# Attention to the 16 meta keys: one joint transpose and one block-diagonal product per block of 128 queries, instead of one small transpose and one small product per head

## The chip, the cores and the metric

The kernel runs on one core of a Trainium2 chip. The metric is the device time of one execution, in microseconds (us); lower is better. A core has TensorE (matmul, in the profile PE, its weight loads PEld), VectorE (DVE), ScalarE (ACT), GpSimd (POOL), and SyncE (SP), which starts most DMAs. Each engine works through its own list in order and waits on semaphores that the others raise.

## The reference

One hybrid decoder layer on 512 tokens of width 1024, with 16 learned meta tokens ahead of them: sliding-window attention (8 query heads, 2 key heads, head size 64, window 128), gated linear attention beside it, a gated merge, and a mixture of 32 experts. The change touches only this part of the attention:

```python
s_band = einsum('bnqhgd,bnkhd->bnhgqk', qb, k_band) * scale     # 128 queries x 256 keys of the band
s_meta = einsum('bnqhgd,bmhd->bnhgqm', qb, k_meta) * scale      # 128 queries x 16 meta keys
p = softmax(concatenate([s_meta, s_band, sink], axis=-1))
o = einsum('bnhgqk,bnkhd->bnqhgd', p_band, v_band) + einsum('bnhgqm,bmhd->bnqhgd', p_meta, v_meta)
```

## The kernel before

The 512 tokens are four blocks (b = 0 to 3) of 128 queries. A pair (b, i) with i = 0 to 3 stands for two query heads j = 0, 1 of block b, one for each key head; there are 16 pairs, numbered n = 4b + i. One list of steps, `SCHEDULE` (L189 to L254), is walked by all the engines, each doing its own part of every step in that order. In the stretch that holds the attention, it lays the steps of the pairs between 24-matmul units of a large projection (chunks 10 to 17 of the weights, two units each, `unit`; their weights are split in two halves by `prep`, ACT L1233 and DVE L1547; their results go through an exponential on ACT, L1320, and `sig` on DVE, L1699 and L1700). For pair n the order is: unit, then `PV` of pair n-2, `S` of pair n, `PT` of pair n-1, sometimes `ogT` and `oT` (transposes of outputs), then `sig`.

- `S` (L838): TensorE multiplies queries by keys, 272 columns for a head (128 keys of the block before, 16 meta keys, 128 own keys, and the meta keys' scores again behind; block 0 has 144). DVE adds the mask and takes the maximum (L1721, L1726). ACT takes the exponential (L1364, L1366) and leaves the head's probabilities in one of four buffers `prob`.
- `PT` (L851): TensorE transposes the probabilities of the two heads, for each head the 128 columns of the block before (L860, not in block 0), the 128 own columns (L861) and the 16 meta columns (L862). ACT copies head 0 out of PSUM (L1378 the band, L1379 the meta part), DVE copies head 1 (L1738, L1739). The meta part goes into `ptm`, a 128x128 tile whose rows 16 to 127 are zero.
- `PV` (L863): per head one product with the values of the block before (L873), one with the own values (L874), one of `ptm` with the meta values (L877), all added up in the head's 64 columns of one PSUM bank. After i = 3, `onorm` scales the block (DVE L1744 to L1749).

PSUM banks are dealt out by `Banks.take` (L129): every family of steps has a ring of banks, and TensorE waits until the earlier use of a bank has been read. The family "T" (L426), which the transposes of `PT` use, has two banks, 5 and 6: head 0 takes one, head 1 the other. ACT takes the exponentials of `S` of pair n before the copies of `PT` of pair n-1, since this is the order of the list.

Of the kernel before, what the change touches and what calls it, by code (L numbers as in the profile page):

```python
# [21 lines left out]
ALU = mybir.AluOpType  # L22
ACT = mybir.ActivationFunctionType
# [4 lines left out]
T = 512  # L28
P = 128
NB = T // P  # L30
KT = D // P
NM = 16
XC = NM + T
HQ, HKV, DH = 8, 2, 64
# [10 lines left out]
SLOT = 64  # L45
# [23 lines left out]
LOGITS = 2 * NG + NE  # L69
# [6 lines left out]
CST = {}  # L76
_o = 0
for _n, _w in (("ident", 128), ("mask", 288), ("cc", NB * DH), ("ss", NB * DH), ("ccm", DH), ("ssm", DH),
               ("slots", SLOT), ("pad", LOGITS), ("att_mask", 128), ("tok", NB + 1)):
    CST[_n] = (_o, _o + _w)  # L80
    _o += _w
NCST = _o
# [2 lines left out]
def shape_tables():  # L85

    c = np.zeros((P, NCST), np.float32)

    def put(name, value):
        a, b = CST[name]  # L90
        c[:value.shape[0], a:b] = value.reshape(value.shape[0], -1)

    i, j = np.arange(P)[:, None], np.arange(P)[None, :]
    put("ident", np.eye(P, dtype=np.float32))
    prev = np.where(j > i, 0.0, NEG)
    own = np.where(j <= i, 0.0, NEG)
    put("mask", np.concatenate([prev, np.zeros((P, NM)), own, np.zeros((P, NM))], 1).astype(np.float32))
    half = DH // 2
    inv = np.float32(10000.0) ** (-(np.arange(half, dtype=np.float32) * np.float32(2.0)) / np.float32(DH))

    def angles(pos):
        a = pos.astype(np.float32)[..., None] * inv
        return (np.concatenate([np.cos(a), np.cos(a)], -1), np.concatenate([-np.sin(a), np.sin(a)], -1))

    cc, ss = angles(NM + np.arange(T).reshape(NB, P).T)
    put("cc", cc)
    put("ss", ss)
    cc, ss = angles(np.arange(NM))
    put("ccm", cc)
    put("ssm", ss)  # L110
    put("slots", np.tile(np.arange(1, SLOT + 1, dtype=np.float32), (P, 1)))
    put("att_mask", ((i <= j) & (i // GC == j // GC)).astype(np.float32))
    pad = np.zeros((P, LOGITS), np.float32)
    pad[:, NG:2 * NG] = -3.0e38
    put("pad", pad)
    put("tok", np.concatenate([np.tile(np.arange(NB, dtype=np.float32) * P - 2 * T, (P, 1)), i.astype(np.float32)], 1))
    return c


# [69 lines left out]
def schedule():  # L189
# [28 lines left out]
    def product(n):  # L218
        b, i = pairs[n]
        return [("PV", b, i)] + ([("onorm", b)] if i == 3 else [])  # L220

    for c in range(10, 18):
        s += [("prep", c + 1)]
        for u in range(2):
            n = 2 * (c - 10) + u
            b, i = pairs[n]
            s += [("unit", c, u)] + (product(n - 2) if n >= 2 else [])
            s += [("S", b, i)] + ([("PT",) + pairs[n - 1]] if n >= 1 else [])
            if i == 2:
                s += [("ogT", b)] + ([("oT", b - 1)] if b >= 1 else [])  # L230
            s += [("sig", c, u)]
    s += [("prep", 19), ("unit", 18, 0)] + product(14) + [("PT",) + pairs[15], ("unit", 18, 1)] + product(15)
    s += [("unit", 18, 2), ("oT", NB - 1), ("unit", 18, 3)]
    s += [("prep", 20)] + [("unit", 19, u) for u in range(4)]
    s += [("prep", 21), ("unit", 20, 0), ("prep", 22), ("unit", 20, 1), ("unit", 20, 2), ("prep", 23), ("unit", 20, 3), ("hi", 24)]
# [22 lines left out]
def layer_kernel(nc, x, meta_tokens, norm1_w, w_in, q_norm_w, k_norm_w, attn_sinks, gla_gate_up, gla_gate_bias,  # L258
                 gla_norm_w, w_attn_branch, w_gla_branch, w_out, norm2_w, router_rows, norm2_rows,
                 expert_w_gate, expert_w_up, expert_w_down, table, triangle, rows_hbm, out):  # L260
    with ExitStack() as ctx:
# [3 lines left out]
        def sem(name):  # L265
            return ctx.enter_context(nc.semaphore(name))
# [19 lines left out]
        def C(name, rows=P):  # L286
            a, b = CST[name]
            return cst[0:rows, a:b]
# [7 lines left out]
        def at(name, offset, shape, dt=F32):  # L296
            size = int(np.prod(shape[1:])) * 4
            assert offset + size <= arena_size, (name, offset, size, arena_size)
            return nc.alloc_sbuf_tensor_at(name, shape, dt, offset=arena_start + offset)
# [43 lines left out]
        vgm = at("vgm", Y + 14 * K1, [NM, 512])  # L343
        oghi = at("oghi", Y, [P, 4, T], F32R)
        oglo = at("oglo", Y + 8 * K1, [P, 4, T], F32R)
        ptm = [at(f"ptm{i}", 81 * K1 + 512 * i, [P, P]) for i in range(2)]
        place = [Y + 16 * K1]

        def more(name, shape, dt=F32):
# [91 lines left out]
        s_set2 = sem("gate_rows_set")  # L441
        s_reset = sem("chunk_starts_set")
        s_vm0 = sem("meta_values_cleared")
        s_pad = sem("meta_probs_cleared")
        s_sumsq = sem("x_squares_summed")
        s_mean = sem("x_means")
        s_rstd = sem("x_rstd")
# [113 lines left out]
        def head_before(n, k):  # L561

            m = n - k
            return (m // 8, m % 8 // 2, m % 2)
# [39 lines left out]
        def _(pe):  # L604
# [71 lines left out]
            for step in SCHEDULE:  # L676
# [174 lines left out]
                elif kind == "PT":  # L851
                    _, b, i = step
                    n0 = 2 * (4 * b + i)
                    for j in range(2):
                        pe.wait_ge(s_prob, n0 + j + 1)
                        ps = banks.take(pe, "T", ("PT", b, i, j))
                        p = prob[(n0 + j) % 4]
                        own = KW if b else 0
                        if b > 0:
                            nc.tensor.transpose(ps[:, 0:128], p[:, 0:128], ident)  # L860
                        nc.tensor.transpose(ps[:, 128:256], p[:, own:own + P], ident)  # L861
                        nc.tensor.transpose(ps[0:NM, 256:384], p[:, P:KW], ident).then_inc(banks.done(("PT", b, i, j)), 1)  # L862
                elif kind == "PV":  # L863
                    _, b, i = step
                    if i == 0:
# [1 line left out]
                    for j in range(2):  # L867
                        pe.wait_ge(*banks.emptied(("PT", b, i, j)))
                        hd = j * 4 + i
                        o = pv[:, hd * DH:(hd + 1) * DH]  # L870
                        vc = slice(j * DH, (j + 1) * DH)
                        if b > 0:
                            nc.tensor.matmul(o, pt[j][:, 0:128], v_tok[:, b - 1, vc], start=True, stop=False)  # L873
                        nc.tensor.matmul(o, pt[j][:, 128:256], v_tok[:, b, vc], start=(b == 0), stop=False)  # L874
                        if i == 0 and b == 0:
                            pe.wait_ge(s_pad, 2)
                        last = nc.tensor.matmul(o, ptm[j][:, :], vm[:, vc],  # L877
                                                start=False, stop=True)
                    last.then_inc(s_pv, 1)
                elif kind in ("oT", "ogT"):  # L880
                    b = step[1]
# [308 lines left out]
        def _(act):  # L1190
# [29 lines left out]
            for step in SCHEDULE:  # L1220
# [147 lines left out]
                elif kind == "PT":  # L1368
# [2 lines left out]
                    act.wait_ge(*banks.filled(name))  # L1371
                    if 4 * b + i:
                        act.wait_ge(s_pv, 4 * b + i)
                    else:
                        act.wait_ge(s_pad, 1)
                    ps = banks.get(name)
                    c0 = 128 if b == 0 else 0
                    nc.scalar.activation(pt[0][:, c0:256], ps[:, c0:256], ACT.Copy)  # L1378
                    nc.scalar.activation(ptm[0][0:NM, :], ps[0:NM, 256:384], ACT.Copy).then_inc(banks.read(name), 1)  # L1379
                elif kind in ("oT", "ogT"):  # L1380
                    b = step[1]
                    act.wait_ge(*banks.filled(step))
# [93 lines left out]
        def _(dve):  # L1476
# [59 lines left out]
            for step in SCHEDULE:  # L1536
# [171 lines left out]
                elif kind == "S":  # L1708
# [3 lines left out]
                    for j in range(2):  # L1712
                        n = 2 * (4 * b + i) + j
                        hd = j * 4 + i
                        name = ("S", b, i, j)
                        st_ = att_stat[:, b % 2, :, hd:hd + 1]
                        width, m0 = keys(b)[1], 0 if b else KW
                        dve.wait_ge(*banks.filled(name))
                        if n >= 4:
                            dve.wait_ge(*banks.filled(("PT",) + head_before(n, 4)))  # L1720
                        nc.vector.tensor_tensor_reduce(out=prob[n % 4][:, 0:width], in0=banks.get(name)[:, 0:width],  # L1721
                                                       in1=C("mask")[:, m0:m0 + width], scale=1.0, scalar=-3.0e38,
                                                       op0=ALU.add, op1=ALU.max, accum_out=st_[:, 0, :])\
                            .then_inc(banks.read(name), 1)
                        dve.wait_ge(*banks.emptied(name))
                        nc.vector.tensor_scalar(st_[:, 1, :], st_[:, 0, :], -SCALE, nsinks[:, hd:hd + 1],  # L1726
                                                ALU.mult, ALU.min).then_inc(s_max, 1)
                elif kind == "PT":
# [2 lines left out]
                    dve.wait_ge(*banks.filled(name))  # L1731
                    if 4 * b + i:
                        dve.wait_ge(s_pv, 4 * b + i)
                    else:
                        dve.wait_ge(s_pad, 2)
                    ps = banks.get(name)
                    c0 = 128 if b == 0 else 0
                    nc.vector.tensor_copy(pt[1][:, c0:256], ps[:, c0:256])  # L1738
                    nc.vector.tensor_copy(ptm[1][0:NM, :], ps[0:NM, 256:384]).then_inc(banks.read(name), 1)  # L1739
                elif kind == "onorm":  # L1740
                    b = step[1]
                    st_ = att_stat[:, b % 2, :, :]
# [179 lines left out]
        def _(pool):  # L1922
# [31 lines left out]
            for step in SCHEDULE:  # L1954
# [18 lines left out]
                elif kind == "krope":  # L1973
# [9 lines left out]
                    for g in range(HKV):  # L1983
# [7 lines left out]
                    rope(m, tabm[:, 0:1, :].to_broadcast([NM, HKV, DH]), tabm[:, 1:2, :].to_broadcast([NM, HKV, DH]),  # L1991
                         view(n_x, NM, HKV), view(n_t, NM, HKV), krm[:, :].rearrange("p (g d) -> p g d", d=DH),
                         NM, HKV, s_krope, 2)
                elif kind == "kT":
                    pool.wait_ge(*banks.emptied("kdm"))
                    for t in ptm:
                        nc.gpsimd.memset(t[:, :], 0.0).then_inc(s_pad, 1)
                elif kind == "qrope":
                    b = step[1]
                    pool.wait_ge(*banks.emptied(("unit", 6, b)))  # L2000
# [89 lines left out]
```

## Time and profile before

| | |
|---|---|
| Median of 3 runs | 671.71 us (671.52 to 671.83) |
| Span of the profiled execution | 669.8 us |
| Median less span (start and end outside the span) | 1.9 us |
| TensorE busy | 650.2 us, 97% |
| TensorE weight loads busy | 466.9 us, 70% |
| VectorE busy | 390.7 us, 58% |
| ScalarE busy | 215.9 us, 32% |
| GpSimd busy | 101.4 us, 15% |

The page gives the span of the profiled execution, not a separate time of its own; the 1.9 us between it and the median of the runs is what lies around the span. In timelines, a row with xN holds N instructions one behind another. A float32 matmul appears as two matmul instructions (x2). Matmuls overlap, so what one costs in a stream is the distance from its start to the start of the next, not its duration.

### The profile page before, as it was taken

How to read it: one execution, taken by the hardware profiler on the slowest of the kernel's cores; microseconds unless marked ns; L12 is line 12 of the kernel's file. 1: busy time of each engine (PE TensorE's matmuls, PEld its weight loads, DVE VectorE, ACT ScalarE, POOL GpSimd, SP SyncE). 2: the span in 40 equal slices, each digit the busy share in tenths (PEclk: the TensorE clock that was granted, in tenths of full speed). 3: DMA queues.
4: the chain of work that ended last, by engine and by line, in shares of the span. 5: the costliest groups of instructions: out<-in, count | busy, mean ns of one | idle time of the engine just before them, and what ended most of it. 6: DMA issues, size and time to landing. Idle time of an engine off the chain costs nothing.

```text
span 669.8 us, 10196 instructions
## 1 busy us (share of the span) xinstructions
PE 650.2 (97%) x3969; PEld 466.9 (70%) x3969; DVE 390.7 (58%) x736; ACT 215.9 (32%) x448; POOL 101.4 (15%) x138
## 2 busy tenths in 40 slices
PE   5799999999999999999989999999999999999998
PEld 3579999988888888888779995354544445453535
DVE  4648335678897878785674667453443535251615
ACT  6346232234534444422435565302020201110112
POOL 3300015899300000000000010110110101010010
PEclk9899999999999999999999999999999999999999
DMA  7432223202232121112345057999999999999943
GB/s 242 147 125 65 64 65 97 92 1 64 79 100 74 60 68 52 68 44 90 126 166 243 33 219 284 381 408 412 401 422 397 423 394 420 407 418 404 417 185 126
DMA packets 49794, 138.72 MB, mean 207 GB/s; under 512 B 6202, under 2 KB 28235, under 8 KB 41556
## 3 DMA queue, kind: packets, MB, share of 16 engines
q1 hardware_dynamic: 47298, 134.37, 52.8%
q0 software_dynamic: 2304, 3.64, 1.5%
q8 instruction: 32, 0.52, 0.3%
q14 instruction: 14, 0.11, 0.1%
q10 hardware_dynamic: 146, 0.07, 0.0%
HBM read 138.62 MB, written 4.19 MB: 213 GB/s over the span
## 4 chain that ended last, share of the span: by engine, by line
PE 87%; DVE 6%; ACT 3%; issue 2%; DMA 1%; POOL 0%; ACTq 0%; DVEq 0%
PE bank L990 16%; PE bank L608 12%; PE bank L609 12%; PE bank L610 12%; PE bank L1004 8%; PE bank L1114 8%; PE bank L850 1%; DVE y_lo L1903 1%; PE bank L1015 1%; PE bank L877 1%; PE bank L874 1%; ACT whi L1233 1%; DVE sig_a L1617 1%; DVE sig_a L1613 1%; DMA wraw<-in_w_out 1%
## 5 line engine op out<-in xcount | busy, mean ns | idle before, releaser
L990 PE MATMUL bank<-w_pair,xgT 128*64 128x512 f32 x512 | 113.8, 596 | 0.0
L990 PEld LDWEIGHTS bank<-w_pair,xgT 128*64 128x64 f32 x512 | 35.2, 137 | 66.4 <-issue 65.4
L1547 DVE TENSOR_TENSOR wlo<-wraw,whi 128x2048 fp32r<-128x2048 f32 (+1 forms) x25 | 56.4, 2258 | 20.3 <-ACT whi L1233 20.3
L608 PE MATMUL bank<-whi,xhi 128*128 128x256 f32 x224 | 64.4, 288 | 0.0
L609 PE MATMUL bank<-wlo,xhi 128*128 128x256 f32 x224 | 63.0, 281 | 0.0
L610 PE MATMUL bank<-whi,xlo 128*128 128x256 f32 x224 | 62.9, 281 | 0.0
L608 PE MATMUL bank<-xhi,whi 128*128 128x512 f32 x152 | 61.4, 404 | 0.0
L609 PE MATMUL bank<-xlo,whi 128*128 128x512 f32 x152 | 60.1, 396 | 0.0
L610 PE MATMUL bank<-xhi,wlo 128*128 128x512 f32 x152 | 59.7, 393 | 0.0
L1004 PE MATMUL bank<-w_pair,hT 128*64 128x512 f32 x256 | 58.1, 595 | 0.0
L1880 DVE SCALAR_TENSOR_TENSOR hg<-bank,pair_w,hs 128x256 f32<-128x256 f32 x16 | 7.7, 483 | 80.6 <-ACT hs L1452 80.6
L1233 ACT ACTIVATE whi<-wraw 128x2048 fp32r<-128x2048 f32 (+1 forms) x25 | 46.6, 1870 | 24.9 <-PE bank L617 11.1
L1452 ACT ACTIVATE hs<-bank 128x256 f32<-128x256 f32 x16 | 6.1, 384 | 135.5 <-PE bank L990 135.5
L1916 DVE TENSOR_TENSOR h<-h,bank 128x512 f32<-128x512 f32 x64 | 41.4, 681 | 7.5 <-PE bank L1114 6.0
L1114 PE MATMUL bank<-y_hi,onehotT 128*128 128x512 f32 x112 | 44.2, 394 | 1.5 <-DVE y_lo L1903 1.5
L1114 PE MATMUL bank<-y_lo,onehotT 128*128 128x512 f32 x112 | 43.7, 390 | 0.0
L1903 DVE TENSOR_TENSOR y_lo<-bank,y_hi 128x512 fp32r<-128x512 f32 x32 | 20.6, 685 | 39.2 <-ACT y_hi L1465 39.2
L608 PEld LDWEIGHTS bank<-whi,xhi 128*128 128x128 f32 x224 | 42.1, 188 | 1.8 <-issue 1.4
L610 PEld LDWEIGHTS bank<-whi,xlo 128*128 128x128 f32 x224 | 42.2, 188 | 0.0
L609 PEld LDWEIGHTS bank<-wlo,xhi 128*128 128x128 f32 x224 | 42.1, 188 | 0.0
L1004 PEld LDWEIGHTS bank<-w_pair,hT 128*64 128x64 f32 x256 | 17.7, 137 | 33.3 <-issue 33.3
L1927 POOL TENSOR_TENSOR pause<-pause 128x1 f32<-128x1 f32 x34 | 6.0, 196 | 223.0 <-PE bank L984 184.1
(331 smaller groups left out, 1330.9 us busy)
## 6 DMA issues: line engine op xcount, KB each, us to landing
w_pair<-in_expert_w_gate SPq DMA_DIRECT2D x32, 1024.0 KB
w_pair<-in_expert_w_up SPq DMA_DIRECT2D x32, 1024.0 KB
w_pair<-in_expert_w_down SPq DMA_DIRECT2D x32, 1024.0 KB, 17.4
wraw<-in_w_in SPq DMA_DIRECT2D x17, 1024.0 KB, 5.6
wraw<-in_w_out SPq DMA_DIRECT2D x4, 1024.0 KB, 5.3
h<-in_x SPq DMA_DIRECT2D x4, 512.0 KB, 5.3
wraw<-in_w_gla_branch SPq DMA_DIRECT2D x2, 1024.0 KB, 5.0
wraw<-in_w_attn_branch SPq DMA_DIRECT2D x2, 1024.0 KB, 5.2
```

The source lines that it names most:

```text
L608: nc.tensor.matmul(ps, lhi(k), rhi(k), start=(k == 0), stop=False)
L609: nc.tensor.matmul(ps, lhi(k), rlo(k), start=False, stop=False)
L610: last = nc.tensor.matmul(ps, llo(k), rhi(k), start=False, stop=(k == kt - 1))
L850: nc.tensor.matmul(ps[:, 0:width], q, k, start=True, stop=True).then_inc(banks.done(("S", b, i, j)), 1)
L990: last = nc.tensor.matmul(tiles[GU_BANK[s]][j * SLOT:(j + 1) * SLOT, :].rearrange("p (f n) -> p f n", f=2), xgT[:, k, s * P + j * SLOT:s * ...
L1004: last = nc.tensor.matmul(tiles[DOWN_BANKS[s][half]][j * SLOT:(j + 1) * SLOT, :], hT[s][:, f, j * SLOT:(j + 1) * SLOT], we[s][j][2][:, f, ...
L1114: last = nc.tensor.matmul(tiles[SCATTER_BANKS[u % 4]][:, :], onehotT[i % 3][s][:, b, :], part[s][:, cols_], start=(s == 0 and part is y_hi ...
L1233: nc.scalar.activation(wh, raw, ACT.Copy).then_inc(s_hi, 1)
L1547: nc.vector.tensor_tensor(wl, raw, wh.bitcast(F32), ALU.subtract).then_inc(s_lo, 1)
L1880: nc.vector.scalar_tensor_tensor(hg[s][:, :], tiles[GU_BANK[s]][:, FF:2 * FF], pair_w[:, 2 * i + s:2 * i + s + 1], hs[s][:, :], ALU.mult, ...
L1903: last = nc.vector.tensor_tensor(y_lo[s][:, cols_], tiles[DOWN_BANKS[s][half]][:, :], y_hi[s][:, cols_].bitcast(F32), ALU.subtract)
L1916: nc.vector.tensor_tensor(h[:, b, cols_], h[:, b, cols_], tiles[bank][:, :], ALU.add).then_inc(s_add[u % 4], 1)
```

## The change

The 16 meta columns of the probabilities are no longer transposed head by head. GpSimd copies them, as each head's probabilities are ready, side by side into `pm` (128 queries x 8 heads x 16). After `PT` of a block's last pair a new step `metaT` transposes `pm` at once (128x128) through a bank of family "T", and ACT copies it to `pmT`. A block-diagonal matrix `vmb` (128 rows for 8 heads x 16 keys, 512 columns for 8 heads x 64) is built once, by a new step `vmeta`: TensorE repeats the meta values in eight groups of 16 rows, DVE multiplies by a 0/1 table. In `PV` of the last pair, one product of `pmT` with `vmb` adds all eight heads' meta part to the whole bank. The bank's accumulation is started by its first matmul alone. The constants table is 136 columns longer. The buffers `ptm` and their clearing go.

```diff
+    def flip(n):
+        b, i = pairs[n]
+        return [("PT", b, i)] + ([("metaT", b)] if i == 3 else [])
...
-            s += [("S", b, i)] + ([("PT",) + pairs[n - 1]] if n >= 1 else [])
+            s += [("S", b, i)] + (flip(n - 1) if n >= 1 else [("vmeta",)])
...
-    s += [("prep", 19), ("unit", 18, 0)] + product(14) + [("PT",) + pairs[15], ("unit", 18, 1)] + product(15)
+    s += [("prep", 19), ("unit", 18, 0)] + product(14) + flip(15) + [("unit", 18, 1)] + product(15)
...  TensorE
-                        nc.tensor.transpose(ps[:, 128:256], p[:, own:own + P], ident)
-                        nc.tensor.transpose(ps[0:NM, 256:384], p[:, P:KW], ident).then_inc(banks.done(("PT", b, i, j)), 1)
+                        nc.tensor.transpose(ps[:, 128:256], p[:, own:own + P], ident).then_inc(banks.done(("PT", b, i, j)), 1)
+                elif kind == "metaT":
+                    b = step[1]
+                    pe.wait_ge(s_pm, 8 * (b + 1))
+                    ps = banks.take(pe, "T", step)
+                    nc.tensor.transpose(ps[:, 0:P], pm[b % 2][:, :, :], ident).then_inc(banks.done(step), 1)
+                elif kind == "vmeta":
+                    pe.wait_ge(*banks.emptied(("unit", 5, "m")))
+                    ps = banks.take(pe, "T", step)
+                    nc.tensor.matmul(ps[:, 0:P], C("copies", NM), vm[0:NM, :], start=True, stop=True).then_inc(banks.done(step), 1)
...
+                        first = i == 0 and j == 0
                         if b > 0:
-                            nc.tensor.matmul(o, pt[j][:, 0:128], v_tok[:, b - 1, vc], start=True, stop=False)
-                        nc.tensor.matmul(o, pt[j][:, 128:256], v_tok[:, b, vc], start=(b == 0), stop=False)
-                        last = nc.tensor.matmul(o, ptm[j][:, :], vm[:, vc],
-                                                start=False, stop=True)
+                            nc.tensor.matmul(o, pt[j][:, 0:128], v_tok[:, b - 1, vc], start=first, stop=False)
+                        last = nc.tensor.matmul(o, pt[j][:, 128:256], v_tok[:, b, vc], start=first and b == 0, stop=False)
+                    if i == 3:
+                        pe.wait_ge(*banks.emptied(("vmeta",)))
+                        pe.wait_ge(*banks.emptied(("metaT", b)))
+                        last = nc.tensor.matmul(pv[:, :], pmT[:, :], vmb[:, :, :].rearrange("p h d -> p (h d)"), start=False, stop=True)
...  ScalarE
-                    nc.scalar.activation(pt[0][:, c0:256], ps[:, c0:256], ACT.Copy)
-                    nc.scalar.activation(ptm[0][0:NM, :], ps[0:NM, 256:384], ACT.Copy).then_inc(banks.read(name), 1)
+                    nc.scalar.activation(pt[0][:, c0:256], banks.get(name)[:, c0:256], ACT.Copy).then_inc(banks.read(name), 1)
+                elif kind == "metaT":
+                    b = step[1]
+                    act.wait_ge(*banks.filled(step))
+                    if b:
+                        act.wait_ge(s_pv, 4 * b)
+                    nc.scalar.activation(pmT[:, :], banks.get(step)[:, 0:P], ACT.Copy).then_inc(banks.read(step), 1)
...  VectorE
+                            dve.wait_ge(s_pm, n - 3)
...
-                    nc.vector.tensor_copy(pt[1][:, c0:256], ps[:, c0:256])
-                    nc.vector.tensor_copy(ptm[1][0:NM, :], ps[0:NM, 256:384]).then_inc(banks.read(name), 1)
+                    nc.vector.tensor_copy(pt[1][:, c0:256], banks.get(name)[:, c0:256]).then_inc(banks.read(name), 1)
+                elif kind == "vmeta":
+                    dve.wait_ge(*banks.filled(step))
+                    dve.wait_ge(*banks.filled(("glao", NB - 1)))
+                    full = [P, HKV, 4, DH]
+                    nc.vector.tensor_tensor(vmb[:, :, :].rearrange("p (g i) d -> p g i d", g=HKV), ...
+                                            ALU.mult).then_inc(banks.read(step), 1)
...  GpSimd
-                elif kind == "kT":
-                    pool.wait_ge(*banks.emptied("kdm"))
-                    for t in ptm:
-                        nc.gpsimd.memset(t[:, :], 0.0).then_inc(s_pad, 1)
+                elif kind == "S":
+                    _, b, i = step
+                    if i == 0 and b >= 2:
+                        pool.wait_ge(*banks.filled(("metaT", b - 2)))
+                    for j in range(2):
+                        n = 2 * (4 * b + i) + j
+                        pool.wait_ge(s_prob, n + 1)
+                        nc.gpsimd.tensor_copy(pm[b % 2][:, 2 * i + j, :], prob[n % 4][:, P:KW]).then_inc(s_pm, 1)
```

## Rows read from the trace of the kernel before

**Rows 1.** Chain of waits, 160 to 350 us, by line; then a piece of it.
```profile
by line: PE bank L608 17.9%; PE bank L609 17.8%; PE bank L610 17.7%; PE bank L850 5.1%; issue 4.3%; PE bank L877 3.8%; PE bank L874 3.6%; ACT whi L1233 3.0%; DVE sig_a L1617 3.0%; DVE sig_a L1613 2.9%; DMA wraw<-in_w_out 2.8%; DVE wlo L1547
...
306.27 1.93 ACT whi L1233
```

**Rows 2.** Stretches: busy us (instructions) of the engines, PEclk, DMA share, GB/s.
```profile
20.00:30.00 10.00, 9.56 (x35) 6.21 (x36) 6.58 (x6) 0.69 (x3) 5.41 (x9) 0.83 0.69 224
...
250.00:300.00 50.00, 50.00 (x288) 41.49 (x286) 42.55 (x68) 20.12 (x54) 0.00 (x0) 1.00 0.15 51
...
330.00:350.00 20.00, 17.27 (x103) 14.71 (x102) 14.88 (x17) 8.95 (x10) 0.00 (x0) 1.00 0.43 145
```

**Rows 3.** Instructions of L877: minimum, median, maximum ns, first and last start.
```profile
L877 PE MATMUL bank<-kvm,ptm x64: 275/275/275, 180.2 to 299.9; 128*128 128x64 f32 x64
```

**Rows 4.** TensorE's timeline, PV, S and PT at pair 8: start, us, instruction.
```profile
228.69 0.39 PE L877 MATMUL bank<-kvm,ptm 128*128 128x64 f32 x2
228.91 0.39 PE L873 MATMUL bank<-v_tok,pt 128*128 128x64 f32 x2
...
229.67 0.73 PE L850 MATMUL bank<-kT,qT 64*128 64x272 f32 x4
...
230.83 0.27 PE L861 MATMUL bank<-cst,prob 128*128 128x128 f32 x1
230.94 0.27 PE L862 MATMUL bank<-cst,prob 128*16 128x128 f32 x1
```

**Rows 5.** TensorE's timeline, a float32 product of 512 columns and what follows.
```profile
45.55 1.12 PE L750 MATMUL bank<-gdT,gate_up 17*128 17x512 f32 x2
46.51 0.51 PE L757 MATMUL bank<-gdT,gate_up 17*128 17x16 f32 x4
```

**Rows 6.** Timeline of DVE and ACT, the same pair 8.
```profile
230.43 0.44 DVE L1721 CUSTOM_DVE_ANT_0 prob<-bank,cst 128x272 f32<-128x272 f32 x1 [0.62 <-PE bank L850]
...
231.17 0.52 ACT L1364 ACTIVATE prob<-prob,att_stat 128x272 f32<-128x272 f32 x1 [2.07 <-DVE att_stat L1726]
...
231.99 0.27 DVE L1739 COPY ptm<-bank 16x128 f32<-16x128 f32 x1
...
232.57 0.36 ACT L1378 ACTIVATE pt<-bank 128x256 f32<-128x256 f32 x1
```

**Rows 7.** Timeline around pair 4: TensorE, DVE at pairs 3, 4 and 5, ACT.
```profile
197.15 0.27 PE L861 MATMUL bank<-cst,prob 128*128 128x128 f32 x1
...
189.34 0.31 DVE L1721 CUSTOM_DVE_ANT_0 prob<-bank,cst 128x144 f32<-128x144 f32 x1 [0.75 <-PE bank L850]
...
196.98 0.44 DVE L1721 CUSTOM_DVE_ANT_0 prob<-bank,cst 128x272 f32<-128x272 f32 x1 [0.36 <-PE bank L850]
...
204.04 0.69 DVE L1749 TENSOR_TENSOR o_tok<-bank,att_stat 128x512 f32<-128x512 f32 x1 [1.39 <-PE bank L877]
...
199.11 0.26 ACT L1378 ACTIVATE pt<-bank 128x128 f32<-128x128 f32 x1
```

**Rows 8.** Timeline at the last pair: TensorE and ACT.
```profile
295.50 0.27 PE L861 MATMUL bank<-cst,prob 128*128 128x128 f32 x1
...
295.60 0.38 ACT L1378 ACTIVATE pt<-bank 128x256 f32<-128x256 f32 x1 [0.74 <-PE bank L862]
```

**Rows 9.** Timeline at 399 us: a weight load that waits for an ACT copy.
```profile
399.40 0.38 ACT L1396 ACTIVATE xnT<-bank 128x256 f32<-128x256 f32 x1 [0.20 <-PE bank L898]
...
399.84 0.52 PEld L909 LDWEIGHTS bank<-router,xnT 128*128 128x128 f32 x4 [0.22 <-ACT xnT L1396]
```

**Rows 10.** TensorE's timeline, two of its idle times.
```profile
20.44 3.56 PE L636 MATMUL bank<-xhi,gdp 128*48 128x512 f32 x8 [3.91 <-DVE xlo L1565]
...
335.13 0.50 PE L608 MATMUL bank<-ohi,whi 128*128 128x512 f32 x1 [1.10 <-DVE sig_g L1613]
```

**Rows 11.** POOL's timeline, two like operations, the second its last for long.
```profile
166.90 3.23 POOL L1927 TENSOR_TENSOR rgs<-og,rgs 128x512 f32<-128x512 f32 x1
...
172.47 1.28 POOL L1927 TENSOR_TENSOR rgs<-og,rgs 128x512 f32<-128x512 f32 x1
```

More of the change, by code:

```diff
@@ L78 @@
 for _n, _w in (("ident", 128), ("mask", 288), ("cc", NB * DH), ("ss", NB * DH), ("ccm", DH), ("ssm", DH),
-               ("slots", SLOT), ("pad", LOGITS), ("att_mask", 128), ("tok", NB + 1)):
+               ("slots", SLOT), ("pad", LOGITS), ("att_mask", 128), ("tok", NB + 1), ("copies", 128), ("own_head", HQ)):
     CST[_n] = (_o, _o + _w)
@@ L116, in shape_tables @@
     put("tok", np.concatenate([np.tile(np.arange(NB, dtype=np.float32) * P - 2 * T, (P, 1)), i.astype(np.float32)], 1))
+    put("copies", (np.arange(NM)[:, None] == j % NM).astype(np.float32))
+    heads = np.arange(HQ)[None, :]
+    put("own_head", (i // NM == 2 * (heads % 4) + heads // 4).astype(np.float32))
     return c
@@ L345, in layer_kernel @@
         oglo = at("oglo", Y + 8 * K1, [P, 4, T], F32R)
-        ptm = [at(f"ptm{i}", 81 * K1 + 512 * i, [P, P]) for i in range(2)]
+        pm = [at(f"pm{i}", 81 * K1 + 512 * i, [P, HQ, NM]) for i in range(2)]
+        vmb = at("vmb", G + 48 * K1, [P, HQ, DH])
+        pmT = at("pmT", G + 50 * K1, [P, P])
         place = [Y + 16 * K1]
@@ L443, in layer_kernel @@
         s_vm0 = sem("meta_values_cleared")
-        s_pad = sem("meta_probs_cleared")
+        s_pm = sem("meta_probs_kept")
         s_sumsq = sem("x_squares_summed")
@@ L871, in _ @@
                         vc = slice(j * DH, (j + 1) * DH)
+                        first = i == 0 and j == 0
                         if b > 0:
-                            nc.tensor.matmul(o, pt[j][:, 0:128], v_tok[:, b - 1, vc], start=True, stop=False)
-                        nc.tensor.matmul(o, pt[j][:, 128:256], v_tok[:, b, vc], start=(b == 0), stop=False)
-                        if i == 0 and b == 0:
-                            pe.wait_ge(s_pad, 2)
-                        last = nc.tensor.matmul(o, ptm[j][:, :], vm[:, vc],
-                                                start=False, stop=True)
+                            nc.tensor.matmul(o, pt[j][:, 0:128], v_tok[:, b - 1, vc], start=first, stop=False)
[4 more added lines that the diff above has]
+                        last = nc.tensor.matmul(pv[:, :], pmT[:, :], vmb[:, :, :].rearrange("p h d -> p (h d)"), start=False, stop=True)
                     last.then_inc(s_pv, 1)
@@ L1373, in _ @@
                         act.wait_ge(s_pv, 4 * b + i)
-                    else:
-                        act.wait_ge(s_pad, 1)
-                    ps = banks.get(name)
                     c0 = 128 if b == 0 else 0
-                    nc.scalar.activation(pt[0][:, c0:256], ps[:, c0:256], ACT.Copy)
-                    nc.scalar.activation(ptm[0][0:NM, :], ps[0:NM, 256:384], ACT.Copy).then_inc(banks.read(name), 1)
+                    nc.scalar.activation(pt[0][:, c0:256], banks.get(name)[:, c0:256], ACT.Copy).then_inc(banks.read(name), 1)
[5 more added lines that the diff above has]
+                    nc.scalar.activation(pmT[:, :], banks.get(step)[:, 0:P], ACT.Copy).then_inc(banks.read(step), 1)
                 elif kind in ("oT", "ogT"):
@@ L1733, in _ @@
                         dve.wait_ge(s_pv, 4 * b + i)
-                    else:
-                        dve.wait_ge(s_pad, 2)
-                    ps = banks.get(name)
                     c0 = 128 if b == 0 else 0
-                    nc.vector.tensor_copy(pt[1][:, c0:256], ps[:, c0:256])
-                    nc.vector.tensor_copy(ptm[1][0:NM, :], ps[0:NM, 256:384]).then_inc(banks.read(name), 1)
+                    nc.vector.tensor_copy(pt[1][:, c0:256], banks.get(name)[:, c0:256]).then_inc(banks.read(name), 1)
[3 more added lines that the diff above has]
+                    full = [P, HKV, 4, DH]
+                    nc.vector.tensor_tensor(vmb[:, :, :].rearrange("p (g i) d -> p g i d", g=HKV),
+                                            banks.get(step)[:, 0:P].rearrange("p (g d) -> p g d", g=HKV).unsqueeze(2).to_broadcast(full),
+                                            C("own_head").rearrange("p (g i) -> p g i", g=HKV).unsqueeze(3).to_broadcast(full),
+                                            ALU.mult).then_inc(banks.read(step), 1)
                 elif kind == "onorm":
```

## The prediction

> **What bounds the kernel now.** I read the page first (busy shares, slices), then the chain of waits, then TensorE's own waits, then the timeline of one pair of heads. TensorE is busy 97% of the span. In the chain from 160 to 350 us the large units' lines L608 to L610 and the attention's L850, L877 and L874 lead, and up to 306 us every piece is TensorE's own [rows 1]: the reader is to see that nothing else releases it there. The stretches say the same: between 250 and 300 us TensorE is busy 50.00 of 50 us, DVE 42.55, ACT 20.12 [rows 2]. So an instruction more or less on TensorE counts in full, and so does any wait that it gets. Behind 306 us the chain hops between ACT, DVE and DMA, but its first hop, ACT L1233, starts when TensorE ends a unit at 306 [rows 1]; all that follows moves with it. I count the sum on this execution's span, 669.8 us; the median of the runs is 1.9 us above it, and I add the change of the span to the median.
>
> **What TensorE loses.** Of L877 there are 64 instructions, so 32 float32 products, one for each head and block [rows 3]; of L862 there is one transpose for each head and block too, 32. In the stream an L877 product takes from 228.69 to 228.91, that is 0.22 us; a transpose of PT takes from 230.83 (L861) to 230.94 (L862), that is 0.11 us [rows 4], and I take the same for the 16-column ones, which repeat at this distance. Removed: 32 x 0.22 = 7.0 and 32 x 0.11 = 3.5, together 10.5 us.
>
> The Trainium skill (TensorE: Matmul & The Clock Gate, Back-to-back issue gap) prices one matmul of N columns at N/2.4 + 2.5 ns, and with four passes for true float32 (FP8 and Floating Point Precision, TensorE Precision Notes) a 64-column product would be 0.12 us; by that estimate only 3.7 us would go in place of 7.0, and the result would be 3.3 us worse. The trace has 0.22 us, since full weights are loaded for each; it decides.
>
> **What TensorE gains in work.** Four wide products, 128x128 by 512 columns in float32. The nearest row is L750, float32 with 512 columns too: 0.96 us to the next start, with the start of another kind of product behind it included [rows 5]. I take 0.9, since the wide product follows its like: 3.6 us. Bounds: 4 x 0.22 (no dearer than an L877) and 4 x 1.12 (L750's full duration), 0.9 to 4.5. Four `metaT` transposes at 0.11 are 0.4 us. `vmeta`, one product with 128 columns, lies between one and two L877 products, 0.2 to 0.5; I take 0.3. Added: 4.3 us. By work alone the change is worth 10.5 - 4.3 = 6.2 us.
>
> **What TensorE gains in waits.** Family "T" has two banks. PT of pair n-1 takes both, head 0 the one that ACT empties, head 1 the one that DVE empties. Until now the next taker was PT of the next pair, a whole unit later, and found them free. `metaT` is a third taker immediately behind: the ring gives it head 0's bank again (13 uses lie ahead of the attention, `vmeta` makes them 14, each pair adds two, so the parity holds; each `metaT` turns the roles of the banks, but still meets head 0's). TensorE must stand until ACT has copied head 0, and ACT comes to that copy only behind both exponentials of S of pair n, which TensorE issued less than a microsecond before.
> At pair 8 [rows 4, 6]: S starts at 229.67, DVE's maximum at 230.43, the exponentials at 231.17 and 231.88, L1378 from 232.57 to 232.93. PT's last L862 would be over at 230.94 + 0.11; with two transposes less, `metaT` wants to start 0.22 earlier, at 230.83. Wait: 232.93 - 230.83 = 2.1 us. From the end of an ACT copy to the weight load that waited for it, 399.78 to 399.84, are 0.06 us [rows 9]; with this and refilling the pipe 2.2 us. None of the pieces between S and L1378 is removed, so the distance stays.
> Pair 12 repeats pair 8's pattern (two such in all): 2.2.
> At pair 4, whose PT is block 0's (two transposes left, so `metaT` wants 197.15), L1378 ends at 199.37 [rows 7]: 2.2, with the restart 2.3. Here DVE has little slack: it waited 0.75 us for S at pair 3 and 0.36 at pair 4 [rows 7]. TensorE comes faster, by 0.66 us for a pair (two L877, two L862), against 0.27 us less work on DVE, L1739 [rows 6]; at pair 3 it is 1.0 us ahead of before (2 x 0.66, less 0.3 for `vmeta`), at pair 4 the gain and DVE's saving and wait cancel, so DVE comes 0.2 to 0.3 us late. So 2.5.
> At the last pair no S lies ahead. `metaT` wants to start where L861 does now, 295.50. L1378 ran from 295.60 for 0.38 us [rows 8] and would start one transpose (0.11) earlier, ending at 295.87. Wait and restart: 0.5.
> Sum of waits: 2.5 + 2.2 + 2.2 + 0.5 = 7.4 us. Bounds: zero, if the bank were free after all, and 4 x 3.3 (from S to the end of L1378 at pair 8), 13.
>
> Behind the standing `metaT` in TensorE's list are the next unit, PV and S, so all wait; nobody makes the time up, since DVE and ACT only feed on what TensorE delivers there. The wide product itself waits for `pmT`, which has a unit of time: no cost.
>
> **The edits that I cost at nothing.** GpSimd's 32 copies: it is idle from 173.8 us on (its last work there, 172.47 and 1.28 us [rows 11]; 0.00 between 250 and 300 us [rows 2]), and the meta columns of a block's last head are ready a whole pair before `metaT` asks. Cover gone, each copy would stand in the path; a POOL operation took 3.23 us once where its like took 1.28 [rows 11], so 2 us more at a `metaT` is the bound, 0 to 8 in all. DVE's new wait for these copies asks for heads four back: free. The 16 small copies less on ACT and on DVE each are hidden by TensorE as it is: 0. `pmT`'s copy on ACT stands a fraction of a microsecond behind `metaT` and delays only L1233, which has a chunk of slack: 0, at most 4 x 0.3. DVE's `vmb` product, 128x512 like L1749's 0.69 us [rows 7], comes at pair 0, and DVE's waits at pairs 1 to 3 take it up: 0, at most 0.7. The constants table grows by 136 x 4 x 128 bytes, 70 KB; at the 224 GB/s of 20 to 30 us [rows 2] that is 0.3 us of DMA that TensorE does not wait for: 0 to 0.3.
>
> **Sum.** -10.5 + 4.3 + 7.4 = +1.2 us; 669.8 becomes 671.0 in the span, 672.9 against the median. The gain in work is used up by the wait at a bank.
>
> **Rivals.**
> (A) The wait is not there, or almost: then only the work counts, -6.2 us, 665.5. Against it: the bank order is fixed by the program, and all pieces ahead of L1378 stand in the timeline. For it: a slip of mine in who frees which bank (head 1's, which DVE frees as L1739 starts, 231.99 [rows 6], would give 1.2 us in place of 2.1, near 669). Chance of either 0.12.
> (B) Slower clearly. A standing TensorE loses its clock. In this trace it stood 3.91 us ahead of 20.44 [rows 10], and from 20 to 30 us the granted clock is 0.83 [rows 2], which is a stretch of 3.4 us at 1.2 GHz in place of 2.4, costing 1.7 us. The gap of 1.10 us ahead of 335.13 [rows 10] left it at 1.00 [rows 2]. A wait of 2.2 us lies between. If each of the three did this: +5.1, so 678.0. It decides from a wait somewhere between 1.1 and 3.9 us on. Chance 0.08.
> The Trainium skill (TensorE: Matmul & The Clock Gate, The HAM clock gate) says just that, an idle TensorE is set back to half its clock; the row at 20 to 30 us agrees, and whether 2.2 us is enough no row shows.
> (C) Longer waits at the same place: DVE, faster driven, arrives later at S than I count, or GpSimd's copies are late: 1 us more at two or three places, 675.5. Chance 0.1.
>
> **How the numbers follow.** The forecast, 672.9, has 0.7; its own range, from the wide product (0.85 to 1.1 us each) and half a microsecond on the waits, is 671.5 to 674.5. What can be told from no change is 0.2%, 1.3 us: 670.4 to 673.05. The forecast case splits into 0.42 within and 0.28 above. With A 0.12 faster (most below 670.4) and B and C 0.18 slower: faster 0.12, same 0.43, slower 0.45. Range for 8 in 10: 669.3 to 675.5, which reaches into A's variant and to C.
>
> **What would show it.** Right: TensorE idle ahead of each `metaT` transpose, about 2.2 us three times and 0.5 once, released by ACT's pt copy; pairs in between shorter by 0.66 us; DVE's idle time before L1721 smaller; a wide product of 0.9 us; the stretch behind 306 us shifted, not changed. Wrong: `metaT` close behind PT with no gap (A), PEclk under 1.00 between 195 and 275 us (B), or gaps of 3 us and more, released by POOL or behind a late DVE (C).

## The result and the profile after

| | before | after |
|---|---|---|
| Median | 671.77 us (4 runs, 671.52 to 672.53) | 678.14 us (4 runs, 675.89 to 678.37) |
| Ratio, after to before | | 1.0086, 95% interval 1.007 to 1.0102 |
| Span of the profiled execution | 669.8 us | 674.1 us |
| TensorE busy | 650.2 us, 97% | 648.0 us, 96% |
| Mean granted TensorE clock | 0.997 | 0.992 (other runs 0.990, 0.987, 0.987) |

The change makes the kernel slower by 0.9%. The forecast was 672.9 with a range to 675.5; the measured median lies outside. The profiled execution, 675.89 us, is the quickest of the four, and time and mean clock go together: 675.89 at 0.992, 677.95 at 0.990, 678.37 and 678.34 at 0.987.

TensorE's waits of the changed kernel, the line with the longest sum (us in total, times, longest):

```profile
PE bank L875 <- ACT pt L1393: 6.7, 4, 2.2
```

L875 is `metaT`. Its four starts in TensorE's timeline (start, us, instruction, idle time before it):

```profile
198.02 0.45 PE L875 MATMUL bank<-cst,pm 128*128 128x128 f32 x1 [2.25 <-ACT pt L1393]
...
233.85 0.30 PE L875 MATMUL bank<-cst,pm 128*128 128x128 f32 x1 [2.08 <-ACT pt L1393]
...
268.57 0.30 PE L875 MATMUL bank<-cst,pm 128*128 128x128 f32 x1 [2.08 <-ACT pt L1393]
...
299.54 0.30 PE L875 MATMUL bank<-cst,pm 128*128 128x128 f32 x1 [0.35 <-ACT pt L1393]
```

So the waits are there, 2.25, 2.08, 2.08 and 0.35 us, and ScalarE's copy of head 0 ends them. For the weight load of the first three `metaT` the profile names GpSimd's copy into `pm` (L2026) in its place. That is the copy for a head of the next block, 197.59 to 197.79 at the first wait; the last one that `metaT` needs there is one of the two from 189.63 on and ended by 190.41. What ACT does ahead of the end of the second wait can be held against [rows 6]:

```profile
231.95 0.52 ACT L1382 ACTIVATE prob<-prob,att_stat 128x272 f32<-128x272 f32 x1 [1.63 <-DVE att_stat L1747]
...
232.65 0.51 ACT L1382 ACTIVATE prob<-prob,att_stat 128x272 f32<-128x272 f32 x1
...
233.34 0.36 ACT L1393 ACTIVATE pt<-bank 128x256 f32<-128x256 f32 x1
```

Both exponentials come first, then the copy, which ends at 233.70, 3.25 us behind the start of S (230.45); in the kernel before it was 3.26 us (229.67 to 232.93). What the forecast did not have is what happened behind the first and the third wait. The large unit's products start, behind the first:

```profile
198.69 0.63 PE L618 MATMUL bank<-xlo,whi 128*128 128x512 f32 x1
199.12 0.63 PE L619 MATMUL bank<-xhi,wlo 128*128 128x512 f32 x1
...
201.51 0.40 PE L619 MATMUL bank<-xhi,wlo 128*128 128x512 f32 x1
201.75 0.39 PE L617 MATMUL bank<-xhi,whi 128*128 128x512 f32 x1
```

They come 0.43 us apart at first and 0.24 us at 201.5. The stretches (columns as in [rows 2]) show the clock beside it:

```profile
198.00:199.00 1.00, 0.98 (x3) 0.90 (x4) 1.00 (x1) 0.28 (x1) 0.00 (x0) 0.50 1.07 360
...
200.00:201.00 1.00, 1.00 (x4) 0.81 (x3) 0.96 (x3) 0.00 (x0) 0.00 (x0) 0.50 0.47 145
...
269.00:270.00 1.00, 1.00 (x5) 0.80 (x4) 1.00 (x1) 0.19 (x1) 0.00 (x0) 0.78 1.05 410
...
195.00:215.00 20.00, 17.75 (x82) 13.16 (x78) 13.90 (x23) 6.69 (x18) 0.79 (x4) 0.91 0.18 54
230.00:240.00 10.00, 7.92 (x43) 6.24 (x43) 6.60 (x12) 2.61 (x10) 0.39 (x2) 1.00 0.34 105
265.00:275.00 10.00, 7.92 (x33) 5.97 (x32) 6.33 (x12) 2.08 (x9) 0.39 (x2) 0.83 0.33 105
```

Behind the first wait the granted clock is 0.50, 1.2 GHz, as soon as TensorE resumes; behind the third it falls about 1 us later (resumed at 268.57, 0.78 from 269 to 270 us). Over 20 us it is 0.91, over 10 us 0.83: (1 - 0.91) x 20 / 0.5 and (1 - 0.83) x 10 / 0.5 both give about 3.5 us at half clock, 1.7 us lost each. Behind the wait at 233.85, as long as that at 268.57, it stayed at 1.00. Two such stretches on top of the forecast's 671.0 are 674.4; the span is 674.1.

### The profile page after: what moved, and what is told of

Same layout as the page of the kernel before. It is cut to its first block, busy times and chain, and to the rows that moved or that the text cites. A ratio compares the mean times of both kernels' runs of the same rounds, so it can differ in the third digit from the quotient of the medians.

```text
span 674.1 us, 10048 instructions
## 1 busy us (share of the span) xinstructions
PE 648.0 (96%) x3887; PEld 460.9 (68%) x3887; DVE 389.5 (58%) x721; ACT 214.5 (32%) x436; POOL 107.8 (16%) x168
## 4 chain that ended last, share of the span: by engine, by line
PE 84%; DVE 8%; ACT 4%; issue 3%; DMA 1%; POOL 0%; ACTq 0%; DVEq 0%
PE bank L1008 16%; PE bank L617 12%; PE bank L618 11%; PE bank L619 11%; PE bank L1022 8%; PE bank L1132 8%; DVE y_lo L1928 1%; PE bank L859 1%; DVE wlo L1567 1%; PE bank L1033 1%; PE bank L961 1%; PE bank L892 1%; PE bank L927 1%; ACT whi L1251 1%; DVE sig_a L1637 1%
## 5 line engine op out<-in xcount | busy, mean ns | idle before, releaser
L1567 DVE TENSOR_TENSOR wlo<-wraw,whi 128x2048 fp32r<-128x2048 f32 (+1 forms) x25 | 56.4, 2258 | 19.8 <-ACT whi L1251 19.8
L1251 ACT ACTIVATE whi<-wraw 128x2048 fp32r<-128x2048 f32 (+1 forms) x25 | 46.7, 1871 | 25.1 <-PE bank L626 11.1
## 6 DMA issues: line engine op xcount, KB each, us to landing
w_pair<-in_expert_w_up SPq DMA_DIRECT2D x32, 1024.0 KB, 11.3
```

Source lines behind the costliest of these rows:

```text
L1251: nc.scalar.activation(wh, raw, ACT.Copy).then_inc(s_hi, 1)
L1567: nc.vector.tensor_tensor(wl, raw, wh.bitcast(F32), ALU.subtract).then_inc(s_lo, 1)
```

## The experiments

Each is timed beside the kernel before on the same chip: 672.39 us (17 runs, 671.33 to 672.83) for e1 to e4, 671.47 us (15 runs, 670.15 to 672.56) for e5 to e7. Of the 17 runs 6 are near 671.4 us at a mean clock of 0.997 and 11 near 672.5 us at 0.995; the median is one of the second kind. "Idle" is TensorE's. Line numbers are each kernel's own.

**The changed kernel again (e1).** No edit.

> The changed kernel once more, for its own runs beside the others. Theory (a wait for a PSUM bank at each metaT, and TensorE set back to 1.2 GHz behind some of these waits): 673 us plus 1.7 for each stretch at half clock, so 675 to 678.5, and the mean granted clock of a run falls with its time. Rival (the time over 673 has another cause, say GpSimd or DMA): time and granted clock do not go together.

Measured: 676.73 us (675.79 to 679.43) against 672.39; ratio 1.0072 (1.0057 to 1.0088). The profiled run was the slowest, 679.43, at a mean clock of 0.987. Its waits and the same three stretches:

```profile
PE bank L875 <- ACT pt L1393: 7.7, 4, 3.2
...
195.00:215.00 20.00, 16.78 (x67) 12.51 (x64) 12.72 (x23) 6.09 (x17) 0.79 (x4) 0.83 0.17 54
230.00:240.00 10.00, 7.92 (x36) 6.22 (x35) 8.71 (x13) 2.63 (x9) 0.39 (x2) 0.83 0.34 105
265.00:275.00 10.00, 7.92 (x39) 6.20 (x38) 9.74 (x13) 3.75 (x10) 0.39 (x2) 0.91 0.32 105
```

All three long waits went with half clock here (the third stretch crosses the border at 275 us and so shows as 0.91), the first for twice as long: (1 - 0.83) x 20 / 0.5 is 6.8 us, which began at 198.1, 0.8 us before TensorE resumed, so that not all of it was lost work. Four units of 1.7 us, at most 6.8 us, on 671.0 make 677.8; the span is 677.6. In all six runs time and mean clock go together (near 676.0 us at 0.992, 677.45 at 0.990, 678.85 and 679.43 at 0.987). The theory stands; the expected top of 678.5 was a little low.

The first wait was 3.2 us because DVE came 1 us later to S of pair 4, rival C's late DVE at one place. None of the changed steps made it late: DVE was 1.4 us behind the other execution already at `prep` (L1567, 167.94 against 166.50), ahead of the first of them. Three of its instructions between 150 and 159 us took longer here, 1.36 us against 0.29, 3.01 against 2.28 and 1.38 against 0.29; why, no run shows.

**metaT one unit later (e2).** All work of the change stays; only `metaT` moves.

```diff
     def product(n):
-        return [("PV", b, i)] + ([("onorm", b)] if i == 3 else [])
+        return ([("metaT", b)] if i == 3 else []) + [("PV", b, i)] + ([("onorm", b)] if i == 3 else [])
     def flip(n):
-        return [("PT", b, i)] + ([("metaT", b)] if i == 3 else [])
+        return [("PT", b, i)]
```

> metaT moved from behind PT of the last pair to just ahead of PV of the last pair, one unit later, where both banks of family T have long been read; all the work stays. Theory: the four waits for the bank go (7.4 us) and the clock stays up, only the saved work counts: 671.8 - 6.2 = 665.5 us, perhaps 0.2 more at each wide product while pmT is copied. Rival (the saving in work is smaller than counted, since VectorE becomes the bound once TensorE is faster): 668 to 671.

Measured: 666.65 us (666.4 to 667.62); ratio 0.9925 (0.9912 to 0.9938). The saved work counts nearly in full: 5.0 us (4.2 to 5.9) by the ratio, 5.2 by the spans, and 4.8 between runs of the same mean clock, 0.997 (666.6 against 671.4). The 5.7 of the medians flatters it, since it sets runs at 0.997 against a median at 0.995. Span 664.6 against 669.8 - 6.2 = 663.6. TensorE's timeline at the first wide product (L896; `metaT` is L875) shows where part of the difference is:

```profile
200.84 0.27 PE L875 MATMUL bank<-cst,pm 128*128 128x128 f32 x1
...
201.53 0.27 ACT L1399 ACTIVATE pmT<-bank 128x128 f32<-128x128 f32 x1
201.94 1.10 PE L896 MATMUL bank<-vmb,pmT 128*128 128x512 f32 x2 [0.44 <-ACT pmT L1399]
202.97 0.73 PE L859 MATMUL bank<-kT,qT 64*128 64x272 f32 x4
```

In block 0 PV is short and the wide product waits 0.44 us for `pmT`; and the product takes 1.03 us, not 0.9. TensorE also waits 0.6 us, once, for DVE's copy of head 1 (`pt`, L1756), which it did not do in the kernel before: a small part of the rival, DVE as the bound. This version beats both kernels, by more than any other here.

**The wait alone, in the kernel before (e3).**

```diff
                         nc.tensor.transpose(ps[0:NM, 256:384], p[:, P:KW], ident).then_inc(banks.done(("PT", b, i, j)), 1)
+                    if i == 3:
+                        pe.wait_ge(*banks.emptied(("PT", b, i, 0)))
```

> The kernel before, with one thing added: behind PT of each block's last pair TensorE waits until ScalarE has emptied head 0's bank, as metaT does. Theory: 3 waits of 2.1 us and one of 0.5, 6.8 us with the restarts, plus 1.7 us for each stretch at half clock (1 to 3): 680 to 684 us. Rival (the waits cost what they last and the clock has nothing to do with it): 678.6.

Measured: 682.73 us (681.44 to 683.63) against 672.39; ratio 1.0158 (1.0144 to 1.0172), 10.6 us. Waits, and stretches around the first three (2.03, 1.92 and 1.92 us; the last is 0.29):

```profile
PE bank L608 <- ACT ptm L1381: 6.2, 4, 2.0
...
195.00:215.00 20.00, 17.97 (x91) 14.32 (x89) 14.35 (x25) 7.16 (x20) 0.00 (x0) 0.91 0.18 54
230.00:240.00 10.00, 8.08 (x39) 6.30 (x38) 9.04 (x14) 2.65 (x10) 0.00 (x0) 0.83 0.34 105
270.00:280.00 10.00, 8.08 (x39) 6.25 (x38) 6.85 (x13) 2.39 (x9) 0.00 (x0) 0.83 0.32 107
```

6.2 us of idle time and three stretches at 1.7 are 11.3; the span grew by 11.1 (680.9 against 669.8). Nothing of the change is in this kernel, no joint transpose, no GpSimd copies: each of the three waits costs nearly as much again as it lasts.

**The wait filled with work (e4).** Ahead of `metaT`'s bank, in blocks 0 to 2:

```diff
+                        for q in range(9):
+                            nc.tensor.matmul(banks.tiles[nb_][:, :], split(whi, 12 + 2 * b, gd_hi)[:, q % KT, 0:P], xhi[:, q % KT, NM:XC], start=True, stop=True)
                     ps = banks.take(pe, "T", step)
```

> The changed kernel, with nine float32r products of 512 columns into the next unit's bank, whose result is overwritten, put into each of the first three waits (9 x 0.233 = 2.1 us): the wait stays as long, TensorE is busy in it. Theory: no stretch at half clock, 672.9 us (671.0 + 1.9), with little spread over runs. Rival (the spread and the extra microseconds come from something other than the idle engine): as the changed kernel, 676 to 678.

Measured: 672.62 us (671.05 to 673.76); ratio 1.0009 (1.0001 to 1.0018). The same three stretches, in the order of the changed kernel's:

```profile
195.00:215.00 20.00, 19.93 (x103) 15.11 (x103) 15.39 (x27) 7.44 (x20) 0.79 (x4) 1.00 0.18 54
230.00:240.00 10.00, 10.00 (x52) 7.77 (x48) 5.66 (x12) 2.63 (x9) 0.40 (x2) 1.00 0.35 105
265.00:275.00 10.00, 10.00 (x48) 7.62 (x47) 5.46 (x11) 2.63 (x9) 0.40 (x2) 1.00 0.29 107
```

The useless products take the place of the idle time: `metaT` starts 3.25 us behind S at pair 4 (195.32 to 198.57), in the changed kernel 3.35 us (194.67 to 198.02), so 0.1 us a wait is what an engine that need not restart saves. Yet the kernel is 4 to 5.5 us quicker than the changed one (676.73 and 678.14), and 0.3 us from the 672.9 that the forecast had named. All but some 0.3 us of that part of the loss is the clock.

**PT and metaT ahead of S (e5).**

```diff
-            s += [("S", b, i)] + (flip(n - 1) if n >= 1 else [("vmeta",)])
+            if n and i == 0:
+                s += flip(n - 1) + [("S", b, i)]
+            else:
+                s += [("S", b, i)] + (flip(n - 1) if n >= 1 else [("vmeta",)])
```

> The changed kernel, with PT of a block's last pair and metaT put ahead of S of the next pair in the list, so that ScalarE copies head 0 before it has exponentials to do. metaT still takes head 0's bank at once. Theory: three waits of about 0.5 us in place of 2.2 (the last pair's 0.5 stays), no stretch at half clock: 666.5 + 4 x 0.5, 668 to 669 us, and mean clock 0.997. Rival (any wait of TensorE there sets the clock back): 1.7 us more for each, 670 to 674.

Measured: 668.43 us (667.55 to 668.6) against 671.47; ratio 0.9947 (0.9934 to 0.9961). `metaT` is L878 here; TensorE's timeline at pair 8:

```profile
228.66 0.30 PE L878 MATMUL bank<-cst,pm 128*128 128x128 f32 x1 [0.35 <-ACT pt L1396]
228.90 0.73 PE L862 MATMUL bank<-kT,qT 64*128 64x272 f32 x4
```

The wait shrinks from 2.08 to 0.35 us once ACT has no exponentials ahead of the copy. This shows that the order of the list, not the bank alone, made the wait long. The mean clock of the profiled run was 0.995, not 0.997: at the start of the kernel the half-clock stretch was twice as long in this execution; in the attention the clock stayed up.

**The small transposes put back (e6).** On e2:

```diff
-                        nc.tensor.transpose(ps[:, 128:256], p[:, own:own + P], ident).then_inc(banks.done(("PT", b, i, j)), 1)
+                        nc.tensor.transpose(ps[:, 128:256], p[:, own:own + P], ident)
+                        nc.tensor.transpose(ps[0:NM, 256:384], p[:, P:KW], ident).then_inc(banks.done(("PT", b, i, j)), 1)
```

Their result is read by nothing.

> e2_meta_late with the 32 transposes of 16 meta columns put back, whose result nothing reads. It splits the gain in work. Theory: 32 x 0.11 = 3.5 us more than e2_meta_late, 670.2 us. Rival (a transpose with 16 columns is nearly free, its stream being hidden by the weight load behind it): within 1 us of e2_meta_late, 667.5.

Measured: 670.01 us (669.74 to 671.16) against 671.47; ratio 0.9982 (0.9973 to 0.9991). Against e2's 0.9925 that is 0.57% of 672, 3.8 us, for a counted 3.5 (spans: 668.1 - 664.6 = 3.5). So a 16-column transpose cost TensorE the same 0.11 us as a full one here.

**A shorter wait in the kernel before (e7).**

```diff
+                    if i == 3 and b < NB - 1:
+                        pe.wait_ge(s_prob, n0 + 4)
```

> The kernel before, with a wait of TensorE behind PT of the last pair of blocks 0 to 2 for the next pair's second exponential, some 1.4 us each by its timeline (232.4 against 231.05), in place of e3's 2.0. Theory (the clock falls only behind waits that are long enough, and 1.4 us is nearer to 2 than to the 1.1 that left it alone): 4.2 us for the waits and 0 to 2 stretches of 1.7: 676 to 680. Rival (1.4 us never sets it back): 676.3 with the mean clock at 0.997.

Measured: 676.49 us (674.87 to 676.86) against 671.47; ratio 1.0061 (1.0048 to 1.0075), 4.1 us.

```profile
PE bank L608 <- ACT prob L1366: 4.2, 3, 1.5
...
230.00:240.00 10.00, 8.69 (x48) 6.85 (x47) 7.44 (x13) 2.51 (x9) 0.00 (x0) 1.00 0.34 105
```

The rival was right: the waits (1.53, 1.31 and 1.31 us) left the clock alone, and its mean was 0.997 or 1.0 in all five runs. They cost about what they last: 4.2 us of idle time, against 4.1 us by the ratio and 5.2 by the spans; what is between the two the runs leave open. In the profiled executions, no wait of 1.53 us or less in the attention went with half clock, and eight of nine waits of 1.92 us and more did (changed kernel two of three, e1 and e3 three of three each). What decides between them, whether it is the length alone, and why one wait of 2.08 us was spared, no run here tells.

## Why the prediction was wrong

- **What bounds the kernel: right.** Work taken from TensorE counted nearly in full (e2), work that replaced idle time cost nothing (e4), and the stretch behind 306 us only shifted.
- **Removed, 10.5 us: right.** The small transposes were counted 3.5 and measured 3.5 by the spans. From S to S, pair 8 came 8.30 us behind pair 7 before (221.37 to 229.67) and 7.64 us after (222.81 to 230.45), the 0.66 us a pair of the forecast.
- **Added work, 4.3 us: a little low.** The wide product goes from start to start in 1.00 us where S follows:

```profile
205.63 1.08 PE L896 MATMUL bank<-vmb,pmT 128*128 128x512 f32 x2
206.63 0.73 PE L859 MATMUL bank<-kT,qT 64*128 64x272 f32 x4
```

 That is 0.3 us more over these three than counted, inside the bounds; and with `vmeta` S of pair 1 came 6.63 us behind that of pair 0 (167.28 to 173.91), 6.22 before (167.29 to 173.51), 0.4 us for a counted 0.3. The Trainium skill's isolated gap (TensorE: Matmul & The Clock Gate, Back-to-back issue gap), taken four times as in the prediction, would have the removed 64-column products at 0.12 us, an estimate, and e2's gain at 2.9 us. The measured gain of 5.0 us leaves no room for that.
- **The wait for the bank, 7.4 us with restarts: right**, with place, releaser and size: 2.25, 2.08, 2.08 and 0.35 us of idle time, 6.7 in all. Counted as the forecast did, from the start that `metaT` would have had (0.11 us behind the last transpose's, 231.61 at pair 8) to the one it got (233.85), the second is 2.24 us for a forecast 2.2. One variant of rival A was added up wrong: three waits shorter by about 1 us would give 670, not "near 669".
- **The edits costed at nothing: right.** The GpSimd copies took 0.2 us each (median), and those that `metaT` needs had ended long before it stood. DVE's lateness at pair 4, forecast at 0.2 to 0.3 us, was under 0.1 in one execution (S to DVE's maximum 0.84 us, 0.76 before) and 1 us in e1, where it came from ahead of the change.
- **The step that failed is the price of the clock, rival B.** The sum gave what follows the three long waits 0 us beyond a restart. I had the mechanism, its rows (3.91 us of idle time and a clock of 0.83 behind it [rows 2, 10]) and its price, 1.7 us a stretch, and said that it "decides from a wait somewhere between 1.1 and 3.9 us on". I then gave it 0.08, for no row bore on 2.2 us, and ended the range at 675.5, short of B's own 678.0. The runs have full clock behind waits of up to 1.53 us (e7) and half clock behind eight of nine of 1.92 us and more (e3, e1 and the changed kernel), so two to three of the three waits had it, 3.4 to 6.8 us in place of 0. That on 671.0 is the whole of what was measured in the spans, and e4 took just this part away. That B's 678.0 meets the median of 678.14 is in part luck: B has three single stretches in every execution, and the two profiled ones had two and four. A mechanism whose trigger lies inside an interval that the trace leaves open, with the case in its middle, deserved about even chances.

## What to carry to other kernels

Ask of every bank, buffer or slot that a moved or added step takes which engine has to empty it first, and what that engine has ahead of the emptying in its own list. A ring of two banks that gets a third user makes a wait of that length. A wait of TensorE has a second price when it is long enough: here 2 us of idle time cost up to 3.7. Moving the taker to where the bank has been free for long (e2) turned a loss of 4 to 6 us into a gain of 5.

## What the runs showed of the hardware

- A TensorE that stood for 1.92 to 3.22 us in the middle of dense work had its clock at 1.2 GHz around or behind the wait in eight of nine cases, seven times for about 3.4 us and once, at the wait of 3.22 us, for 6.8 us. The fall came between 0.8 us before TensorE resumed (e1, first wait) and 1.1 us after (e1, third wait). The waits of 1.31, 1.31 and 1.53 us of e7 did not do it.
- The same kernel differs between runs in the number of these stretches, and with them in time: 675.8 to 679.4 us for the changed kernel in e1, 666.4 to 667.6 for e2, where only the stretch at the start is left. That one is 3.4 us long in the profiled executions of most kernels and twice as long in those of e4 and e5.
- A GpSimd copy of 128x16 float32 took 0.2 us (median of 32, the longest 0.48), and the VectorE reciprocal beside which one ran at 197.6 us kept the 3.35 us that it has in the kernel before.
